# Folding the norm's scale vector into the gate weights of the per-layer embedding, and letting ScalarE write the first two normalised tiles

## What is computed

```
h = h + rms_norm(f, ffn_post_g[i])
gate = jax.nn.sigmoid(rms_norm(h, ple_norm_g[i]) @ w_ple_gate[i])
h = h + (p[i] @ w_ple_proj[i]) * gate
```

## Time and profile before

| | |
|---|---|
| median of 3 runs | 1983.5 us (1981.51 to 1984.2) |
| the profiled execution | 1981.24 us, its span 1979.5 us |
| PE busy | 97% of the span |
| DVE busy | 72% |
| ACT busy | 46% |
| POOL busy | 24% |

### The profile page before, as it was taken

How to read it: one execution, slowest core, us unless ns; L and a number is a source line. 1 busy time by engine, 2 the same in 40 slices (tenths; PEclk the granted TensorE clock), 3 DMA queues, 4 the chain that set the end, 5 groups by cost and what they waited for, 6 DMA issues and landing times.

```text
span 1979.5 us, 28867 instructions
## 1 busy us (share of the span) xinstructions
PE 1926.8 (97%) x9262; PEld 1581.6 (80%) x9262; DVE 1432.1 (72%) x2388; ACT 910.7 (46%) x1738; POOL 465.4 (24%) x464
## 2 busy tenths in 40 slices
PE   7899999999999999999999998999999999999998
PEld 7778888888888878888866687788888888888787
DVE  6987777777777786576578658777777777777863
ACT  5644444444444453343268645444444344444531
POOL 3312222222212221010036311222122221212310
PEclk9999999999999999999999999999999999999999
DMA  5333332233333340231000113233322323335201
GB/s 210 107 96 102 93 92 85 84 91 95 101 95 90 117 176 14 67 112 53 0 12 2 59 49 112 80 96 101 95 90 81 95 78 101 95 100 182 96 27 69
DMA packets 214761, 173.29 MB, mean 88 GB/s; under 512 B 8608, under 2 KB 196384, under 8 KB 214688
## 3 DMA queue, kind: packets, MB, share of 16 engines
q1 hardware_dynamic: 213104, 166.60, 26.5%
q10 hardware_dynamic: 1584, 5.77, 0.8%
HBM read 159.75 MB, written 12.58 MB: 87 GB/s over the span
## 4 chain that ended last, share of the span: by engine, by line
PE 86%; DVE 8%; POOL 2%; issue 2%; DMA 1%; ACT 1%; DVEq 0%; ACTq 0%; POOLq 0%
PE ps L787 14%; PE ps L788 13%; PE ps L789 13%; PE ps L295 7%; PE ps L297 7%; PE ps L296 7%; PE ps L885 7%; PE ps L886 7%; PE ps L884 7%; POOL probs L1633 1%; PE ps L356 1%; DVE ps L1598 1%; PE ps L1587 1%; PE ps L1641 1%; PE ps L593 1%
## 5 line engine op out<-in xcount | busy, mean ns | idle before, releaser
L1209 DVE TENSOR_TENSOR H<-H,ps 128x512 f32<-128x512 f32 x496 | 328.0, 686 | 112.8 <-PE ps L886 111.9
L1071 POOL TENSOR_TENSOR s_raw<-s_raw,a_raw 128x512 f32<-128x512 f32 x66 | 87.5, 1327 | 767.5 <-DVE s_lo L1122 650.7
L787 PE MATMUL ps<-t_hi,s_hi 128*128 128x512 f32 x528 | 206.3, 391 | 6.2 <-DVE t_lo L1221 3.1
L789 PE MATMUL ps<-t_hi,s_lo 128*128 128x512 f32 x528 | 205.5, 389 | 0.0
L788 PE MATMUL ps<-t_lo,s_hi 128*128 128x512 f32 x528 | 205.5, 389 | 0.0
L960 ACT ACTIVATE m<-ps 128x512 f32<-128x512 f32 x44 | 26.4, 601 | 265.7 <-PE ps L789 263.3
L788 PE MATMUL ps<-b_lo,a_hi 128*128 128x512 f32 x352 | 137.0, 389 | 0.0
L787 PE MATMUL ps<-b_hi,a_hi 128*128 128x512 f32 x352 | 137.0, 389 | 0.0
L789 PE MATMUL ps<-b_hi,a_lo 128*128 128x512 f32 x352 | 136.9, 389 | 0.0
L884 PE MATMUL ps<-wd_hi,d_ab_hi 128*128 128x512 f32 x336 | 130.7, 389 | 0.0
L885 PE MATMUL ps<-wd_lo,d_ab_hi 128*128 128x512 f32 x336 | 130.7, 389 | 0.0
(11 more groups left out here) (292 smaller groups left out, 5139.4 us busy)
## 6 DMA issues: line engine op xcount, KB each, us to landing
a_raw<-in_w_ff_gate SPq DMA_DIRECT2D x88, 256.0 KB, 3.0
a_raw<-in_w_ff_up SPq DMA_DIRECT2D x88, 256.0 KB, 3.0
s_raw<-in_w_ff_up SPq DMA_DIRECT2D x88, 256.0 KB, 3.0
s_raw<-in_w_ff_gate SPq DMA_DIRECT2D x88, 256.0 KB, 3.0
wd_raw<-in_w_ff_down SPq DMA_DIRECT2D x44, 512.0 KB, 4.2
residual_spill<-H SPq DMA_DIRECT2D x16, 512.0 KB, 2.6
raw<-in_w_ple_gate SPq DMA_DIRECT2D x16, 512.0 KB, 4.6
back<-residual_spill SPq DMA_DIRECT2D x16, 512.0 KB, 4.8
```

The source lines that it names most:

```text
L787: pe.matmul(ps[:, bank, :], w[0], x[0], start=fresh and k == 0, stop=False, skip_group_check=not fresh)
L789: last = pe.matmul(ps[:, bank, :], w[1], x[0], start=False, stop=k == 3, skip_group_check=not fresh)
L1071: eng.tensor_tensor(form_raw(name), W_RAW[name][:, :, :], form_raw(other) if other != "A21" else W_RAW["A21"][:, :, :], op).then_inc(summe ...
L1209: dve.tensor_tensor(dst, dst, src, ALU.add).then_inc(F["summed"], 1)
```

## The change

- `ple_gain`, a new buffer of 128 x 8 elements, holds `ple_norm_g` with the channel on the partition: block k is column k. ACT issues its load at the start of each layer's feed-forward network, behind `ffn_act_first`. The row load of `gain` at line 1980 goes, and with it a wait for `late_form`.
- The gate weights are cut with the factor in them: hi is the rounded `raw * ple_gain`, by ACT with a scale operand of one element for each partition, and lo is `raw * ple_gain - hi` in one `scalar_tensor_tensor` of DVE.
- The normalised tile is only `H * rstd`. Tiles 2 to 7 are written by DVE (`scaled`, a `tensor_scalar`). Tiles 0 and 1 are written by ACT (`scaled_act`): tile 0 between the last `d_copy_u` and `gate_cut(1)`, tile 1 behind `gate_cut(5)`. Both `normed` calls leave DVE's list.
- New waits for `gain_loaded` stand ahead of the first use of `ple_gain` on ACT and DVE.

```diff
+        def cut_hi_scaled(act, base, j, dst, columns):
+            s, value = loaded(base, j)
+            act.wait_ge(s, value)
+            width = D // len(columns)
+            for n, scale in enumerate(columns):
+                last = act.activation(dst[:, n, :], raw[(base + j) % SLOTS][:, n * width:(n + 1) * width], ACT.Copy,
+                                      scale=scale)
+            last.then_inc(hi_done, 1)
+        def cut_lo_scaled(dve, base, j, dst_hi, dst_lo, columns):
...
+                last = dve.scalar_tensor_tensor(out=dst_lo[:, n, :], in0=raw[(base + j) % SLOTS][:, n * width:(n + 1) * width],
+                                                scalar=scale, in1=dst_hi[:, n, :].bitcast(F32), op0=ALU.mult,
+                                                op1=ALU.subtract)
...
+        def scaled(dve, s, i, p):
+            dve.wait_ge(s["rstd"][p], s.done("rstd", i))
+            dve.tensor_scalar(xn[p][:, :], H[:, tile(i, p)], rstd[p], None, ALU.mult).then_inc(s["xn"][p], 1)
+        def scaled_act(act, s, i, p):
+            act.wait_ge(s["rstd"][p], s.done("rstd", i))
+            act.activation(xn[p][:, :], H[:, tile(i, p)], ACT.Copy, scale=rstd[p]).then_inc(s["xn"][p], 1)
...
@@ ACT, ffn(L)
                 ffn_act_first(act, L)
+                if L == 1:
+                    act.wait_ge(w_ready, BASE["ple0"] + KD)
+                act.dma_start(ple_gain[:, :], I["ple_norm_g"][L].rearrange("(k p) -> p k", p=P),
+                              allow_slow_non_contiguous=True).then_inc(gain_loaded, 16)
                 ffn_act_second(act, L, 0)
...
-                act.wait_ge(F["late_form"], 4 * (L + 1))
-                gain_row(f"ple{L}", I["ple_norm_g"][L])
                 tile_squares(0)
                 for j in range(2):
                     d_copy_u(act, L, last, 1, j)
+                scaled_act(act, s_ple, 0, 0)
                 gate_cut(1)
...
                 gate_cut(5)
+                scaled_act(act, s_ple, 0, 1)
...
@@ DVE, ffn(L)
-                    if k == 5:
-                        dve.wait_ge(gain_loaded, 16 * GAIN[f"ple{L}"])
-                        normed(dve, s_ple, 0, 0)
...
+                dve.wait_ge(gain_loaded, 16 * GAIN[f"ple{L}"])
                 d_los(dve, L, last, 0)
...
                 gate_cut(3)
-                normed(dve, s_ple, 0, 1)
...
-                                (2, third_tile), (2, lambda i, p: normed(dve, s, i, p)),
+                                (2, third_tile), (2, lambda i, p: scaled(dve, s, i, p)),
```

More of the change, by code:

```diff
@@ L291, in cut_lo @@
                               ALU.subtract).then_inc(w_ready, 1)
+        def cut_hi_scaled(act, base, j, dst, columns):
[7 more added lines that the diff above has]
+        def cut_lo_scaled(dve, base, j, dst_hi, dst_lo, columns):
+            dve.wait_ge(hi_done, base + j + 1)
+            width = D // len(columns)
+            for n, scale in enumerate(columns):
+                last = dve.scalar_tensor_tensor(out=dst_lo[:, n, :], in0=raw[(base + j) % SLOTS][:, n * width:(n + 1) * width],
+                                                scalar=scale, in1=dst_hi[:, n, :].bitcast(F32), op0=ALU.mult,
+                                                op1=ALU.subtract)
+            last.then_inc(w_ready, 1)
         def product(pe, out_, lhs, rhs, first, last):
@@ L571, in row_load @@
             eng.dma_start(dst[:, :], src.partition_broadcast(P)).then_inc(s, 16)
+        ple_gain = sb("ple_gain", [P, KD])
         GAIN = {"ffn0": 1, "ple0": 2, "kv": 3, "q": 4, "ffn1": 5, "ple1": 6}
@@ L1959, in gate_cut @@
                 def gate_cut(k):
-                    cut_hi(act, BASE[f"ple{L}"], k, w_pg[0][:, k, :])
+                    cut_hi_scaled(act, BASE[f"ple{L}"], k, w_pg[0][:, k:k + 1, :], [ple_gain[:, k:k + 1]])
                 def tile_squares(p):
@@ L1967, in ffn @@
                 gate_silu(act, L, last, 1, 1)
+                act.wait_ge(gain_loaded, 16 * GAIN[f"ple{L}"])
                 row_load(act, post_gain, I["ffn_post_g"][L], post_gain_loaded)
@@ L2150, in gate_cut @@
                 def gate_cut(k):
-                    cut_lo(dve, BASE[f"ple{L}"], k, *[w[:, k, :] for w in w_pg])
+                    cut_lo_scaled(dve, BASE[f"ple{L}"], k, *[w[:, k:k + 1, :] for w in w_pg], [ple_gain[:, k:k + 1]])
                 def between(k):
```

## The result

| | median of the runs | lowest to highest | runs |
|---|---|---|---|
| before | 1982.18 us | 1981.48 to 1984.36 | 7 |
| after | 1988.87 us | 1987.53 to 1992.31 | 7 |

A forecast was written before the change was run, and what follows sets the result against it. PE, busy 97% of the span, was taken as the bound, so only its idle time could change. Two layers at +0.24 us, together +0.5 us, on the median of 1983.5 gave 1984.0 us, range 1981.0 to 1987.0.

The forecast's parts named there:

- The edits without a price: Tiles 2 to 7, the row load's removal and new waits cost 0; block cuts on DVE take +0.06 us each.
- The price of a scale operand on ACT: A per-partition scale operand adds 0.08 us to an ACT copy, with bounds 0 and 0.08.
- First place: DVE's last add, which lets PE start the gate products, comes 0.87 us later, with PE's start at 730.09.
- Second place: Weight block 3 is ready 0.99 us later, and PE waits some 0.55 us there.
- Third place: Normalised tile 1: POOL's factor at 735.88, `scaled_act` from 735.93, PE's transpose at 737.12, +0.79 us.
- What is given back: After tile 1's transpose PE has everything, with no wait behind the gate products, leaving +0.24 us.
- Rival 4: Longer idle time before the gate products lowers the granted clock: 5.5 us on top, 1989.5 us; chance 0.02.
- The sum: Both layers +0.24 us each, together +0.5 us, between -0.2 and +0.5 by the operand.
- The new load: The load of 1024 single elements on ACT issues in some 0.4 to 0.6 us, drains in 2.5, costs 0.
- rival 1: The load of single elements holds ACT: at 6.18 us it costs 6.0 us in all, 1989.5 us; chance 0.07.

The follow-up runs named there:

- e1: The changed kernel, with DVE made to wait for POOL's factor of tile 1 before it cuts weight block 4; 1983.99 us, ratio 1.0003.
- e8: The changed kernel, with two more DVE instructions ahead of block 4's cut, each with one operand in PSUM; 1982.05 us, ratio 0.9996.
- e4: The kernel before, with DVE cutting weight blocks 4 and 5 ahead of normalising tile 1 instead of after; 1987.26 us, ratio 1.0022.
- e3: The changed kernel, with 16 filler matmuls on PE in the wait ahead of tile 1's transpose; 1985.70 us, ratio 1.0016.
- e6: The kernel before, with only the load of single elements added on ACT's queue, into a buffer nobody reads; 1982.88 us, ratio 0.9998.

## Why the prediction was wrong

**The edits without a price, right.** The 80 us of later tiles are still gapless, 80.00 of 80.00, with DVE at 39.69 instead of 44.67; `tensor_scalar` takes 0.75 us instead of 1.28:

```profile
L373 DVE TENSOR_SCALAR xn<-H,small x12: 752/753/755, 754.8 to 1951.0; 128x1024 f32<-128x1024 f32 x12
...
L299 ACT ACTIVATE w_ple_gate_hi<-raw,ple_gain x16: 1135/1139/1142, 713.9 to 1873.2; 128x1024 fp32r<-128x1024 f32 x16
...
L377 ACT ACTIVATE xn<-H,small x4: 1141/1144/1147, 725.9 to 1871.1; 128x1024 f32<-128x1024 f32 x4
```

**The price of a scale operand on ACT, right in size.** ACT's copies with the operand take 1.14 us where those without took 1.05: 0.09, for 0.08 taken. The bound of 0 is out. The Trainium skill (ScalarE: Activation LUTs, What ACT_TABLE_LOAD costs) gives about 93 ns for such an operand, and the trace agrees, with its 90.

**First place, right.** Forecast 730.09 for PE's start, measured 733.60 - 3.48 = 730.12; `slot_lo` is released by ACT's `xt_hi`, as was said.

**Second place, right.** A wait of 0.50 us for block 3 where 0.55 was forecast, and 1.02 us later than before where 0.99 was.

**Third place: the step that failed.** "POOL's factor at 734.95 + 0.93 = 735.88." The squares came when they should (737.35 - 3.48 = 733.87 for 733.84). Then the step shifted POOL's two instructions as if their durations were their own. They belong to what DVE does beside them: the factor was there at 741.27 - 3.48 = 737.79, 1.91 us late, and `scaled_act` (737.82 for 735.93) and the transpose (739.02 for 737.12) with it, 1.9 each. The prediction itself had written down that DVE would run its cuts through this time, as something "given back", and took DVE's 1.03 us of waiting for a loss that the change removes. It was the quiet in which POOL could finish. e1, which puts nothing but that quiet back, and e8, which fills it with DVE work of another kind, show it; e4 makes the same loss without the change. What the step needed stood in the prediction: its own cuts of blocks 4 and 5 start at 734.9 and 736.1 and end at 736.18 and 737.38, and POOL's two instructions end 0.05 and 0.42 us behind such ends, the second at 737.80 instead of 735.88.

**What is given back, right in mechanism, and a little more than counted.** There is no wait ahead of the projection. From the transpose to the projection I had reckoned 743.83 - 737.12 = 6.71 us, so 6.94 to its second matmul; at full clock that distance is 6.64 in e3 and 6.66 in e1, 0.3 less. The reckoning took over a wait that it did not see, since the busy transposes hide it:

```profile
737.46 0.50 PE L295 MATMUL ps<-w_ple_gate_hi,xt_hi 128*128 128x512 f32 x1
```

In before the first product behind the transposes starts 1.13 us after them (736.33), when DVE has just cut block 4 (736.19 + 1.22 = 737.41); in e1 and e3 it starts 0.85 after them.

**Rival 4, the mechanism that the forecast gave 0.02.** The clock did fall, not ahead of the gate products but behind the wait for tile 1, and for 3.4 us in each layer. Its price, "1.4 us more" for a block, was near: 1.59 us a layer. What was wrong is its chance and its condition: it was weighed for the wait as forecast, and with the third place wrong the wait was 2.33 us instead of some 0.5. The chance also rested on a misreading. A 9 in the row of 40 slices means 90% or more, not full speed, and before has such a fall itself, in the pooling, at a wait of 2.68 us (the window, then PE's row; the same transposes take 1.09 us where the clock is full):

```profile
85.00:95.00 10.00, 7.32 (x37) 6.86 (x36) 9.62 (x14) 6.10 (x9) 0.74 (x2) 0.66 0.69 235
...
88.49 1.76 PE L485 MATMUL ps<-ident,tmp 128*128 128x128 f32 x7 [2.68 <-DVE tmp L474]
```

So the clock is a second term of the same error: it came in with the long wait.

**The sum.** Forecast +0.24 us a layer; to it come +1.90 by POOL, +1.59 by the clock and -0.30 by the distance just told: +3.43, as measured in layer 0. Both layers: 6.7 us for 0.5.

**The new load, and rival 1.** The issue took 0.39 us, and the transfer landed after 2.2 us. PE's wait in the network's first group, said to stay at 0.93, was 1.23 in after's profile; with the same load it was 0.84 in e6 and 0.99 in e1, so this is scatter about the old value. The drain was estimated at 2.5 us. The Trainium skill (DMA: Bandwidth & Descriptors, Specifications and Rules for kernel authors) warns of one descriptor for each element, and of pieces under 512 B. No run here shows what such pieces cost in bandwidth; for these 4 KB e6 shows no cost to the kernel.

**A rule that would have caught it.** The Trainium skill says (SBUF — State Buffer, Who interferes with whom) that a DVE instruction with two SBUF inputs contends with a GpSimd instruction that reads SBUF, while one with at most one SBUF input, outside its two-port modes, does not. By the Trainium skill (SBUF — State Buffer, Summary: rules for kernel authors), the one of the two that issues second waits until the first has finished. The traces agree where DVE came first: 1.14 and 1.48 us for 0.19 and 0.55 beside the cuts, 0.19 and 0.55 beside the operand from PSUM (e8). Where POOL came first they show no such wait: in before DVE's cut at 725.02 took its usual 1.22 us though POOL's 0.55 us at 724.82 had not ended.

## What to carry to other kernels

Before taking away a wait, look at what runs on the other engines while it lasts: if a tiny instruction on POOL lies on the path to PE, its duration may be that of a quiet DVE. What it becomes without the quiet is to be seen at other executions of the same line (here 1.60 us against 0.55): the rest of the DVE instruction in progress and a little more. When an instruction moves from one engine to another, list who is now free to start in its place, and where a wait on PE grows to 2 us or so, as here, name the clock as a possible second cost. A wait put in by hand, which holds its own engine for 1 us (0.97 in e1) and nothing that PE needs, can be the cheapest part of an edit. And look at the granted clock in windows of some 10 us, not only in the 40 slices of the page.

## What was not expected of the hardware

- A POOL instruction on one element per partition takes 0.19 or 0.55 us. If a DVE instruction that reads two tensors from SBUF is in progress when it starts, it ends some 0.05 us (the first kind) or 0.42 us (the second) behind the end of that instruction: 1.0 to 1.6 us in all where it started early in one of 1.2 to 1.3 us. An operand of DVE in PSUM leaves it at 0.19 and 0.55 (e8, and before at 756.99).
- After a wait of 2.3 us PE's matmuls ran at a step of 0.43 us instead of 0.23, with the lower level granted for 3.4 us, at a cost of 1.59 us; behind an equal wait in e4's layer 1 they did not. Why one and not the other stays open.
- A load of 1024 single elements was issued in 0.39 us and had landed after 2.2 us, no slower than the network's loads of 256 KB (3.0 us in the median).
